# A hybrid encoder layer on one core: norms tile by tile, gate loads ahead of their stage, a cache tile for each DMA, the sample tile in the second block, and a third of the weights' low parts on GpSimd

## The reference

```
h = x + 0.5 * post1(SwiGLU_1(pre1(x)))              # D 1024, D_FF 2816
u = pre_mix(h); z = u @ w_in                        # 1024 x 5376: q k v | r k v w a g | gates
A = differential attention (4 heads, rotary, chunk mask; samples read 1024 cached keys each)
B = RWKV-7 time mixing (8 heads of 64, state carried along the tokens)
m = sigmoid(gA) * (A @ w_o_att) + sigmoid(gB) * (B @ w_o_rwkv)
h = h + post_mix(m @ w_out)
y = h + 0.5 * post2(SwiGLU_2(pre2(h)))
```

## Time and profile before

| | before |
|---|---|
| median of 3 runs | 3202.61 us (3199.3 to 3205.78) |
| profiled execution | 3202.13 us, span 3200.4 us |
| PE busy | 3028.9 us (95%) |
| DVE / ACT / POOL busy | 1735.0 / 1265.1 / 473.9 us |
| granted TensorE clock | 0.977 |

### The profile page before, as it was taken

One profiled execution on the slowest core, in us unless ns is written; L12 is line 12 of the kernel. 1 busy time (PEld: TensorE's weight loads), 2 busy tenths in 40 slices (PEclk: granted clock), 3 DMA queues, 4 the chain that ended last, 5 costly groups with the idle time before them and its releaser, 6 DMA issues.

```text
span 3200.4 us, 58193 instructions
## 1 busy us (share of the span) xinstructions
PE 3028.9 (95%) x23816; PEld 2683.5 (84%) x23816; DVE 1735.0 (54%) x2957; ACT 1265.1 (40%) x2494; POOL 473.9 (15%) x609
## 2 busy tenths in 40 slices
PE   7999999998999999999989998999999999999997
PEld 7998999887877878878777787878787889999996
DVE  4455544545344446365676646566575665446444
ACT  4434334434333333343434434443343443344332
POOL 0000000003115133150502304040220100000000
PEclk9999999999999999999989999999999999999998
DMA  5445444566447555352554635342433564445443
GB/s 154 126 128 158 152 128 145 181 198 213 140 150 222 171 184 166 110 157 86 191 167 146 185 115 191 106 144 78 134 117 120 195 206 152 126 145 168 125 128 113
DMA packets 499623, 481.74 MB, mean 151 GB/s; under 512 B 28563, under 2 KB 401708, under 8 KB 499342
## 3 DMA queue, kind: packets, MB, share of 16 engines
q1 hardware_dynamic: 472846, 389.16, 39.5%
q0 software_dynamic: 26512, 88.86, 8.7%
HBM read 430.72 MB, written 48.18 MB: 150 GB/s over the span
## 4 chain that ended last, share of the span: by engine, by line
PE 78%; DVE 9%; DMA 4%; issue 4%; ACT 2%; POOL 2%; SPq 0%; DVEq 0%; ACTq 0%; POOLq 0%
PE ps L246 36%; PE ps L256 27%; PE ps L969 4%; DVE wlo L211 2%; DMA att<-in_cache_att_v_dram 1%; PE ps L1657 1%; PE ps L1739 1%; DVE as L1906 1%; PE ps L1723 1%; PE ps L961 1%; DMA gt<-gates_scratch 1%; ACT whi L203 1%; PE ps L1668 1%; PE ps L268 1%; ACT att L1805 1%
## 5 line engine op out<-in xcount | busy, mean ns | idle before, releaser
L211 DVE TENSOR_TENSOR wlo<-raw,whi 128x512 fp32r<-128x512 f32 x1140 | 818.5, 721 | 901.5 <-ACT whi L203 900.0
L203 ACT ACTIVATE whi<-raw 128x512 fp32r<-128x512 f32 x1140 | 712.7, 629 | 684.2 <-PE ps L246 381.1
L246 PE MATMUL ps<-xnhi,whi 128*128 128x384 f32 x2688 | 930.1, 346 | 18.6 <-DVE xnlo L534 6.9
L246 PE MATMUL ps<-xnhi,wlo 128*128 128x384 f32 x2688 | 906.6, 337 | 0.0
L246 PE MATMUL ps<-xnlo,whi 128*128 128x384 f32 x2688 | 906.3, 337 | 0.0
L246 PEld LDWEIGHTS ps<-xnhi,whi 128*128 128x128 f32 x2688 | 510.5, 190 | 45.5 <-issue 15.5
L246 PEld LDWEIGHTS ps<-xnlo,whi 128*128 128x128 f32 x2688 | 510.9, 190 | 2.3 <-issue 1.9
L246 PEld LDWEIGHTS ps<-xnhi,wlo 128*128 128x128 f32 x2688 | 510.3, 190 | 0.0
L256 PE MATMUL ps<-whi,hidhi 128*128 128x512 f32 x936 | 379.6, 406 | 6.4 <-DVE xnlo L534 4.4
L256 PE MATMUL ps<-whi,hidlo 128*128 128x512 f32 x936 | 367.6, 393 | 0.0
L256 PE MATMUL ps<-wlo,hidhi 128*128 128x512 f32 x936 | 367.5, 393 | 0.0
(11 more groups left out here) (295 smaller groups left out, 3236.2 us busy)
## 6 DMA issues: line engine op xcount, KB each, us to landing
raw<-in_ffn_w_in_dram SPq DMA_DIRECT2D x528, 256.0 KB, 2.9
raw<-in_ffn_w_out_dram SPq DMA_DIRECT2D x264, 256.0 KB, 2.8
raw<-in_w_in_dram SPq DMA_DIRECT2D x252, 256.0 KB, 3.0
xt<-h_scratch SPq DMA_DIRECT2D x36, 512.0 KB, 6.0
att<-in_cache_att_k_dram POOLq DMA_DIRECT2D x32, 512.0 KB, 5.8
att<-in_cache_att_v_dram POOLq DMA_DIRECT2D x32, 512.0 KB, 4.5
rw<-zr_scratch POOLq DMA_DIRECT2D x51, 256.0 KB, 6.8
raw<-in_w_out_dram SPq DMA_DIRECT2D x48, 256.0 KB, 3.0
```

The source lines that it names most:

```text
L203: act.activation(B["whi"][:, slot], B["raw"][:, slot], ACT.Copy).then_inc(E["whi"], 1)
L211: dve.tensor_tensor(B["wlo"][:, slot], B["raw"][:, slot], B["whi"][:, slot].bitcast(F32), ALU.subtract).then_inc(E["wlo"], 1)
L246: ins = pe.matmul(ps[:, bank, 0:BT], B["w" + wt][:, n % RING, i * P:(i + 1) * P], x(xt, i), start=first and i == 0 and (wt, xt) == passes[ ...
```

## The change

1. `TILE_OF` puts the sample tile fourth, first of block 1. Block 0 of attention then has three prompt tiles, block 1 the samples and two prompt tiles.
2. `weights_dve` becomes `weights_low`, run by two engines: slabs with n % 3 == 2 get their low part from GpSimd, the other two thirds from DVE.
3. Norms work tile by tile: squares in halves of 512 columns into a scratch of their own (junk), the first halves before the stage's last slabs; power, scale and add are one tile for each slab slot. The gain is loaded six slabs before the stage ends, since gB is free of the squares.
4. Gate loads 0 and 1 of an OP stage are issued six and five slabs before the stage.
5. The cache goes through six buffers of one tile, with a load of 256 KB for each (128 loads, 64 before); the V part of a sample takes three steps (two before), the start of the samples (Z) three steps (one before), and the turning of the attention weights (T) a step for each chunk.
6. At the start SP issues the x tiles first, PE turns them tile by tile into all eight PSUM banks, three slabs are split ahead of the first use, the first slab's matmuls wait for one part of x each, and everything that is needed late is loaded by GpSimd and finished at slabs 20 to 28.
7. Small ones: -sin is no longer a constant table, the post norm's factor 0.5 sits in the power.

```diff
-TILE_OF = [8, 0, 1, 2, 3, 4, 5, 6, 7]
+TILE_OF = [0, 1, 2, 8, 3, 4, 5, 6, 7]
...
+def by_pool(n):
+    return n % 3 == 2
+
+def low_part(E, n):
+    return (E["wlo_pool"], n // 3 + 1) if by_pool(n) else (E["wlo"], n + 1 - (n + 1) // 3)
...
-def weights_dve(dve, B, E):
+def weights_low(eng, B, E, mine, sem):
     for n in range(FIRST[-1]):
-        slot = n % RING
-        dve.wait_ge(E["whi"], n + 1)
-        dve.tensor_tensor(B["wlo"][:, slot], B["raw"][:, slot], B["whi"][:, slot].bitcast(F32), ALU.subtract).then_inc(E["wlo"], 1)
+        if mine(n):
+            slot = n % RING
+            eng.wait_ge(E["whi"], n + 1)
+            eng.tensor_tensor(B["wlo"][:, slot], B["raw"][:, slot], B["whi"][:, slot].bitcast(F32), ALU.subtract).then_inc(E[sem], 1)
         yield
...
-POST_STEPS, PRE_STEPS = 7, 5
+POST_STEPS, PRE_STEPS, POST_LEAD = 15, 8, 6
...
+        last = k + 1 == len(STAGES)
...
+        def scale(tl):
+            dve.wait_ge(E["rstd"], 3 * (posts + pres) + tl + 1)
+            dve.wait_ge(E["gain_in"], 16 * (posts + 1))
+            dve.scalar_tensor_tensor(B["yb"][:, tl], B["yb"][:, tl], rstd[:, tl:tl + 1], B["gB"][:, :], ALU.mult, ALU.mult).then_inc(E["scaled"], 1)
...
+        for step in range(POST_STEPS - POST_LEAD - 2):
+            if last:
+                if step < NT:
+                    scale(step)
+                    add(step)
+            elif step < NT:
+                scale(step)
+            elif step < 2 * NT:
+                add(step - NT)
+            yield
...
-                events[start[STAGES.index(("OP", oi))] + max(u, 2 * u - 1)].append("gates")
+                events[start[STAGES.index(("OP", oi))] + (2 * u - 1 if u > 1 else u - 6)].append("gates")
...
+            src = t["cache_att_k" if what == 0 else "cache_att_v"][b, kt * P:(kt + 1) * P]
+            pool.dma_start(Z["kv"][:, i % KV], src).then_inc(E["z_ld%d" % (i % KV)], 16)
...
-                norm += [start[k + 1] + i for i in range(POST_STEPS)]
+                norm += [start[k + 1] - POST_LEAD + i for i in range(POST_STEPS)]
...
-                weave({"norm": norm, "rw": rw_pool(pool, B, E, t), "att": att_pool(pool, B, E, t), "late": late(pool, E)}, 1, AHEAD)
+                weave({"weights": weights, "norm": norm, "rw": rw_pool(pool, B, E, t), "att": att_pool(pool, B, E, t), "late": late_pool(pool, B, E)}, 1, AHEAD, False, AHEAD)
```

More of the change, by code:

```diff
@@ L76, in __init__ @@
     def __init__(self, ids):
-        self.free = deque((b, None, 0) for b in ids)
-        self.at = {}
+        self.free = deque((b, "xlo", b + 1) for b in ids)
+        self.at = {("x", 0, kk): kk for kk in range(KT)}
     def take(self, name):
@@ L788, in norm_act, with square @@
     sums = B["small"]
+    squares = 0
+    def square(src, tl, hf):
+        if squares:
+            act.wait_ge(E["squared"], squares)
+        act.activation(B["junk"][:, :], src, ACT.Square, accum_out=sums[:, 30 + 2 * tl + hf:31 + 2 * tl + hf]).then_inc(E["squared"], 1)
     for what, k in norm_sequence():
@@ L805, in norm_act @@
-        for tl in range(NT):
-            if what == "pre":
-                act.wait_ge(E["xin%d" % tl], 16 * (posts + pres))
-                src = B["xt"][:, tl]
-            else:
+            yield
+            for tl in range(NT):
+                if tl == 0 and posts + pres:
+                    act.wait_ge(E["mean_sq"], 3 * (posts + pres))
+                act.wait_ge(E["xin%d" % tl], 16 * (posts + pres + 1))
+                for hf in TWO:
+                    square(B["xt"][:, tl, hf * 512:(hf + 1) * 512], tl, hf)
+                    squares += 1
+                yield
@@ L819, in norm_act @@
+                square(B["yb"][:, tl, hf * 512:(hf + 1) * 512], tl, hf)
+                squares += 1
+                yield
+        posts += 1
+        for _ in range(POST_STEPS - POST_LEAD - 3):
             yield
@@ L912, in rw_counts @@
         for p in range(TILES):
-            names = head.split() + (sample if p == 0 else prompt).split()
+            names = head.split() + (sample if p == SAMPLE else prompt).split()
             if p == PAIRS - 1:
@@ L1705, in att_pe @@
     for n, (blk, h, tile) in enumerate(UNITS):
+        if n == BEFORE:
+            yield from sample()
         first, last_of_head = head_units(n)
@@ L1929, in att_dve @@
         yield "X"
-        yield "T"
+        for c in chunks_of(tile):
+            yield "T"
         yield "V"
@@ L2011, in att_pool @@
     for n, (blk, h, tile) in enumerate(UNITS):
+        if n == BEFORE:
+            yield from sample()
+            pool.wait_ge(E["att_st%d" % blk], 16)
         first, last_of_head = head_units(n)
@@ new lines, with late_pe, late_act @@
+LATE_AT = (20, 22, 24, 26, 28)
+LATE_LOADS = 15
+def late_pe(pe, B, E):
+    pe.wait_ge(E["late_in"], 16 * LATE_LOADS)
+    pe.wait_ge(E["xlo"], KT)
+    yield
+    yield
+    yield
+    pe.wait_ge(E["set"], 4)
+    pe.wait_ge(E["lam_s"], 3)
+    pe.matmul(B["ps"][:, 6, 0:1], B["gt"][0:1, 1024:1024 + P], B["gt"][0:1, 517:518], start=True, stop=True).then_inc(E["lam_mm"], 1)
+    yield
+    pe.wait_ge(E["lam_in"], 1)
+    pe.wait_ge(E["mask_in"], 1)
+    yield
+def late_act(act, B, E):
+    act.wait_ge(E["late_in"], 16 * LATE_LOADS)
+    yield
+    act.wait_ge(E["lam_s"], 2)
+    act.activation(B["gt"][0:1, 514:516], B["gt"][0:1, 512:514], ACT.Exp).then_inc(E["lam_e"], 1)
+    yield
+    yield
+    yield
+    act.wait_ge(E["lam_in"], 1)
+    act.wait_ge(E["mask_in"], 1)
+    yield
@@ L2216, in weave @@
     for name in gens:
-        assert name == "late" or next(gens[name], "end") == "end", name
+        assert next(gens[name], "end") == "end", name
 def program(nc, t):
@@ L2268, in _ @@
             def _(sp):
-                first = init_sp(sp, B, E, t)
-                next(first)
                 norm = norm_sp(sp, B, E, t)
```

861 lines of the change are left out of this document (449 added, 412 removed).

## The result

| | before | after |
|---|---|---|
| median | 3200.95 us (3197.7 to 3205.78) | 3230.82 us (3222.59 to 3232.22) |
| ratio, 95% interval | | 1.0087 (1.0065 to 1.0109) |
| span of the profiled execution | 3200.4 us | 3230.4 us |
| granted clock | 0.977 | 0.973 |

A forecast was written before the change was run, and what follows sets the result against it. PE was taken as the bound, busy 95% of the span, with idle and low-clock time outside the F stages. Terms -9 -6 -33 -31 -8 +18 = -69 took 3202.1 to 3133 us; range 3098 to 3185.

The forecast's parts named there:

- A third of the low parts to GpSimd, -8 and +18: Side work: relief of DVE's queue gains 8 us; PE's waits for GpSimd and contention cost 18.
- PE waits for what GpSimd does in between: RWKV tiles: low parts come late behind GpSimd's loads and mixes, +13 us over nine waits.
- Contention: DVE beside GpSimd: 0.27 us for each of 380 low parts, 103 us of DVE's relief, 5 us on the path.
- rival 2: Shared port: DVE's two-input operations wait a full 1.5 us for GpSimd, +24 us, 3165 us; chance 0.10.
- I take 8: Side work: fewer low parts on DVE shorten the queue ahead of combinations PE awaits, 8 us gained, between 0 and 20.
- Rivals 3 and 4: GpSimd's low parts late once a tile (+60, 3193 us, chance 0.10) or three times (+124, 3257 us, chance 0.07).
- The sample tile in block 1: 0: Side work: the same steps in another order, PE's work unchanged, 0 us, between -10 and +15.
- Start, -9: Kernel's start: x first in the queue and one part enough, first slab at 15.5 for 24.46 us, 9 us gained.
- End, -6: After the last matmul: gain already loaded, squares half done, last add at 3189.3 for 3195.5 us, 6 us gained.
- Cache, -25 idle, -8 clock: Cache loads tile by tile: 27.3 us of PE's waits fall to 2, and 8 us of low-clock time go.
- OP stages, -31: Three OP stages: early gates and norms by tile win 23 us idle and 8 us clock, two thirds of the loss.
- Small items, 0: Priced together with the sample tile's move: no row for gain or loss, 0 us, between -10 and +15.

The follow-up runs named there:

- 5: Both undone (sample tile in first block, DVE makes all low parts), plus GpSimd waiting for every third slab's high part, doing nothing: 3158.76 us, ratio 0.9877.
- 13: Against 6, GpSimd's reading operation behind each wait replaced by three memsets, which read nothing: 3181.55 us, ratio 0.9929.
- 6: Against 5, behind each wait GpSimd also subtracts 128 x 480 numbers of a constant tile into its own tile: 3204.96 us, ratio 1.0015.
- 2: Against the changed kernel, sample tile back in the first block; GpSimd keeps a third of the low parts: 3200.53 us, ratio 0.9998.
- 9: Against the changed kernel with all low parts on DVE, attention's second block ends at slab 668 for 689: 3155.71 us, ratio 0.986.
- 8: Against 3, attention's steps of the last block begin at slab 692 for 686, same end: 3166.83 us, ratio 0.9901.
- 3: Against the changed kernel, both undone: sample tile back in the first block, all low parts on DVE: 3146.51 us, ratio 0.9822.
- 11: Against 3, the first gates of each OP stage load at their slabs again instead of six slabs ahead: 3142.7 us, ratio 0.9821.
- 14: Against 11, the 108 operations of the RWKV's mixes move from GpSimd to DVE: 3132.64 us, ratio 0.9778.

## Why the prediction was wrong

The step that failed is the one under **A third of the low parts to GpSimd, -8 and +18**. Net +10 was forecast for it; it measured +53 to +60, which is about half of the 97 us between the forecast -69 and the measured +28. In its parts:
- *"PE waits for what GpSimd does in between"* (+13) looked at one direction only, the low part that is late behind GpSimd's work. After the change no such wait is left among PE's. What happened is the reverse: GpSimd's work is late behind its low parts. Each of them waits for a high part that ACT can make only when PE frees a slot, so GpSimd could no longer start the RWKV's loads ahead of time (5: +13 to +18 us), and its 1.3 us each push the chains through it back (13: +17 to +21).
- *Contention*: DVE's total came out near the forecast (103 and 114 us, 0.27 and 0.30 for each low part), but by luck. The 0.27 us was one meeting, in which DVE's low part began 0.44 us before GpSimd's mix ended. It ended 0.55 us behind the mix, and so do 24 of the 25 low parts of DVE in that trace that begin over 0.2 us before the end of a 128 x 512 mix, after 0.97 to 1.80 us (alone they take 0.69). So the earlier trace rows already showed a hold to the end of GpSimd's operation, and rival 2's "the rows show 0.27, not 1.5" read it as a small one. The 0.30 us is a mean over few long holds. The term "5 us on the path" was the one that failed: 21 to 28 us. Some holds fall on chains of small dependent operations that PE waits for, 0.16 us becoming 1.18.
- *"I take 8"* for relief: 5 are left, with what the handover costs already off (6 against 2).

Rival 2, the shared port, was the right mechanism for this term but priced at 24 us, by 0.15 a low part that no row gave, and given 0.10. It had nothing of GpSimd's own lateness, which is more than half of the cost (5 and 13). Rivals 3 and 4 saw GpSimd late, but priced waits of PE for low parts, and these didn't come. The Trainium skill (SBUF — State Buffer, section "SBUF: two separate sides") calls the pair of ports of DVE and GpSimd an exclusive lock for the whole instruction, taken by whichever starts first, against DVE operations in a two-port mode, or with two SBUF inputs where GpSimd's operation reads SBUF. These runs agree: L547 with two SBUF inputs grew, L559 with one in PSUM did not, and in 13 the memsets, which read nothing, left the same operation at 0.55 us in all 42 meetings. They did hold up a DVE operation with one SBUF input, six times (0.75 us alone, 1.02 here):

```profile
267.10 2.04 POOL L238 MEMSET own<- 128x480 bf16 x3 [0.23 <-ACT whi L204]
267.69 1.02 DVE L902 TENSOR_SCALAR xt<-xt,small 128x1024 f32<-128x1024 f32 x1
```

The second step that failed is **The sample tile in block 1: 0**, "the same steps in another order", between -10 and +15. It measured +25 to +28. About half of it (9) to most of it (8) is the table of steps that follows from the move, in slabs where the sample tile has no work.

The rest of the change was forecast at -79 and measured -57 (3). Its own terms, from the traces of 3 and before:
- *Start, -9*: -9.1. The first slab starts at 15.36 us (14.88 in the kernel after), forecast 15.5, before 24.46. (The x tile stood behind ten small loads, not nine.)
- *End, -6*: -4.8. In the kernel after the last add ends 11.4 us behind the last matmul (forecast 10, before 16.4). A tile takes 3.06 us there, not 2.39: the power of the next tile, on GpSimd, is itself held up by DVE's scale and add, and the next scale waits for it.

```profile
3216.52 1.29 DVE L895 SCALAR_TENSOR_TENSOR yb<-yb,small,gB 128x1024 f32<-128x1024 f32 x1 [0.78 <-POOL small L862]
3216.73 1.12 POOL L860 TENSOR_SCALAR small<-small 128x1 f32<-128x1 f32 x1
```

  Elsewhere this L860 takes 0.19 us; here it ends 0.05 us behind DVE's scale.
- *Cache, -25 idle, -8 clock*: the waits fell from 27.3 to 2.3 us, as forecast. But slabs 300 to 564 are only 13.6 us shorter. Their idle time fell by 17 us only, so 8 us of other waits came in, and the time at 1.2 GHz rose by 10 us instead of falling by 16. Taking the longest waits away gave none of the clock's share back here; why the granted clock fell at other places was not traced.
- *OP stages, -31*: -16 (slabs 564 to 596 +1.7, 812 to 844 -12.2, 844 to 876 -5.1). The clock loss of 12 that its sum starts from has no row: PE is busy for 31 us at 1.2 GHz in the three windows, of which half is 15.5. "With the gates six slabs early the first is gone": the wait is gone, but the six slabs are not the reason (11). What the 16 us are owed to stays open: the xt loads behind the first gate, or the norms by tile. PE's waits for the pre norm's scaled tile (L859 before) fell from 11.9 to 1.1 us, but only 4.9 of them were behind the start. Undoing either alone was not tried.
- *Small items, 0*: slabs 596 to 812 are 10.6 us shorter, which no term had. That may be the norms or a luckier table, as 8 shows such tables to be worth 20 us; it stays open.

Right, but hidden by the two failures: F stages unchanged, and PE's waits free of the cache's. The waits of some 10 us for GpSimd's low parts did not come, and the waits for DVE's combination grew, which the prediction had named as a sign of being wrong.

## What to carry to other kernels

Moving work to an idle engine is priced in three places: its own time, what it must now wait for in a queue that ran free before, and what it does to the engine it shares a port with. The last is not a mean but a hold to the end of the other's instruction: read a meeting in a trace by how far behind the other's end an operation ends, not by how much longer it took. It counts where an operation that the critical engine waits for is held; so look for two-input GpSimd work beside such chains and try taking it away before adding any (14 gained where the change lost). A table that spreads steps over slabs is itself worth 20 us here: compare a moved item at the same table, or the table's share is put down to the item.

## What the runs showed of the hardware

- A DVE operation with two SBUF inputs that starts while GpSimd runs a two-input operation of 256 or 512 columns is held to its end, whatever its own size. In the kernel after, two columns end 0.02 us behind GpSimd's low part (alone 0.16 us), 384 columns 0.42 (0.55), 512 columns 0.55 (0.69) and 1024 columns 1.08 (1.22). GpSimd's powers of one column hold no low part of DVE: 15 that began beside one took 0.69 us.
- DVE's operations with an input in PSUM keep their time (553 ns x132 in both kernels). GpSimd's memsets, 1140 of 0.50 us, leave DVE's busy total within 2.5 us, but hold a DVE scale of 1024 columns with one SBUF input (0.75 us becoming 1.02).
- It works the other way too: a GpSimd operation of one column takes 1.12 us instead of 0.19 behind a DVE scale of 1024 columns.
- 380 such GpSimd operations cost DVE 114 us; taking 108 out gave it about 53 us back.
